# A two-block transformer kernel: row sums from the residual's addition, squared deviations from ScalarE

## What is computed

```python
def rmsnorm(x, w):
    xf = x.astype(jnp.float32)
    y = xf * lax.rsqrt(jnp.mean(xf * xf, axis=-1, keepdims=True) + EPS)
    return (y * w.astype(jnp.float32)).astype(x.dtype)

def _layer_norm(x, g, b):
    xf = x.astype(jnp.float32)
    mu = jnp.mean(xf, -1, keepdims=True)
    xc = xf - mu
    var = jnp.mean(xc * xc, -1, keepdims=True)
    y = xc * lax.rsqrt(var + NORM_EPS) * g.astype(jnp.float32) + b.astype(jnp.float32)
    return y.astype(x.dtype)

    for l in range(DEPTH_2):
        x = _layer_norm(alpha * x + 0.5 * _swiglu(x, ffn_w_gu[l, 0], ffn_w_down[l, 0]), ln_g[l, 0], ln_b[l, 0])
        ...
        x = _layer_norm(alpha * x + mix, ln_g[l, 1], ln_b[l, 1])
        x = _layer_norm(alpha * x + 0.5 * _swiglu(x, ffn_w_gu[l, 1], ffn_w_down[l, 1]), ln_g[l, 2], ln_b[l, 2])
```

## Time and profile before

| | |
|---|---|
| median of three runs | 1430.88 us |
| the profiled execution | 1435.12 us |
| its span | 1433.5 us |
| TensorE busy | 1351.0 us, 94% |
| VectorE busy | 917.1 us, 64% |
| ScalarE busy | 725.6 us, 51% |
| GpSimd busy | 93.7 us, 7% |
| mean granted clock of TensorE | 0.968 |

### The profile page before, as it was taken

The page is one execution under the profiler, slowest core; times in us unless marked ns, Lnnn a source line. Parts: engine busy times, 40 slices in busy tenths (PEclk is TensorE's granted clock), DMA queues, the critical chain, the costliest instruction groups (busy, mean ns, idle before and its releaser), DMA issues.

```text
span 1433.5 us, 20478 instructions
## 1 busy us (share of the span) xinstructions
PE 1351.0 (94%) x8221; PEld 1193.1 (83%) x8222; DVE 917.1 (64%) x1342; ACT 725.6 (51%) x1142; POOL 93.7 (7%) x137
## 2 busy tenths in 40 slices
PE   6888899998899999999899999999999999899997
PEld 6777888886788888888888888888888888888886
DVE  4787776777656658555666567656667464666556
ACT  5566455554455553564354554555553653354452
POOL 1233000000000000510000000000001400000000
PEclk9997999999999999998999999999999997999999
DMA  7333476665575664432476665666654332375661
GB/s 231 94 113 103 123 214 208 206 185 172 152 219 177 183 188 113 142 118 63 120 235 182 198 204 151 181 203 202 182 162 128 97 118 64 113 235 177 197 200 44
DMA packets 301191, 229.17 MB, mean 160 GB/s; under 512 B 13083, under 2 KB 283818, under 8 KB 301098
## 3 DMA queue, kind: packets, MB, share of 16 engines
q1 hardware_dynamic: 301082, 227.88, 52.8%
q10 hardware_dynamic: 16, 0.00, 0.0%
HBM read 226.80 MB, written 1.05 MB: 159 GB/s over the span
## 4 chain that ended last, share of the span: by engine, by line
PE 70%; DVE 15%; ACT 9%; DMA 3%; issue 2%; POOL 1%; SPq 0%; DVEq 0%; ACTq 0%
PE bank L849 20%; PE bank L783 11%; PE bank L852 10%; PE bank L784 10%; PE bank L785 10%; DVE lo_gu L1665 5%; ACT hi_gu L1316 4%; PE bank L1221 3%; DMA st_dn<-in_ffn_w_down 2%; PE bank L1190 2%; DVE lo_dn L1670 2%; PE bank L1201 1%; DVE conv L1830 1%; DVE stats L1692 1%; DVE n L1715 1%
## 5 line engine op out<-in xcount | busy, mean ns | idle before, releaser
L849 PE MATMUL bank<-xT,hi_gu 128*128 128x512 f32 x1616 | 404.8, 393 | 4.9 <-DVE lo_gu L1665 4.3
L1665 DVE TENSOR_TENSOR lo_gu<-st_gu,hi_gu 128x2048 fp32r<-128x2048 f32 (+2 forms) x146 | 323.4, 2218 | 111.9 <-ACT hi_gu L1316 111.8
L849 PEld LDWEIGHTS bank<-xT,hi_gu 128*128 128x128 f32 x1616 | 297.0, 189 | 64.4 <-DVE lo_gu L1665 6.4
L1316 ACT ACTIVATE hi_gu<-st_gu 128x2048 fp32r<-128x2048 f32 (+3 forms) x147 | 270.2, 1843 | 0.5 <-DMA st_gu<-in_ffn_w_gu 0.3
L852 PEld LDWEIGHTS bank<-xT,lo_gu 128*128 128x128 f32 x1616 | 220.8, 191 | 15.9
L852 PE MATMUL bank<-xT,lo_gu 128*128 128x256 f32 x1616 | 225.5, 282 | 0.0
L783 PE MATMUL bank<-hi_dn,actTh 128*128 128x512 f32 x436 | 172.4, 395 | 9.2 <-DVE actTl L1842 4.7
L784 PE MATMUL bank<-lo_dn,actTh 128*128 128x512 f32 x436 | 170.8, 392 | 0.0
L785 PE MATMUL bank<-hi_dn,actTl 128*128 128x512 f32 x436 | 169.7, 389 | 0.0
L1833 DVE TENSOR_TENSOR act<-act,bank 128x256 f32<-128x256 f32 x101 | 42.6, 421 | 174.2 <-ACT act L1413 174.2
L1323 ACT ACTIVATE hi_dn<-st_dn 128x1024 fp32r<-128x1024 f32 x109 | 114.6, 1056 | 67.9 <-DMA st_dn<-in_ffn_w_down 67.9
(11 more groups left out here) (270 smaller groups left out, 1823.7 us busy)
## 6 DMA issues: line engine op xcount, KB each, us to landing
st_gu<-in_ffn_w_gu SPq DMA_DIRECT2D x176, 512.0 KB, 5.2
st_dn<-in_ffn_w_down SPq DMA_DIRECT2D x109, 512.0 KB, 6.6
st_gu<-in_w_in SPq DMA_DIRECT2D x23, 1024.0 KB, 5.4
st_gu<-in_w_out SPq DMA_DIRECT2D x12, 1024.0 KB, 5.1
st_gu<-in_ffn_w_gate SPq DMA_DIRECT2D x21, 512.0 KB, 4.2
st_gu<-in_ffn_w_val SPq DMA_DIRECT2D x21, 512.0 KB, 5.5
st_gu<-in_w_in SPq DMA_DIRECT2D x10, 512.0 KB, 4.1
gb<-in_ln_g SPq DMA_DIRECT2D x6, 512.0 KB, 7.3
```

What stands on the lines that cost most here:

```text
L849: pe.matmul(b[:, :], hv[:, w, k, :], xT[:, k, :, :].rearrange("p a b -> p (a b)"), start=k == 0, stop=k == KD - 1, skip_group_check=True)
L1316: i = act.activation(high, staged, ACT.Copy)
L1665: i = dve.tensor_tensor(low, staged, high.bitcast(F32), ALU.subtract)
```

## The change

The statistics of norms 1 to 8 are computed in another way:

- `add` also writes the row sum of its half (`accum_out=row_sum`).
- A new step `centre` waits for the second half's sum and, in a layer norm, makes minus_mean of both.
- `bn_stats` and `bn_aggr` fall away for these norms. A new function `deviation` on ScalarE squares both halves of x, with minus_mean as the bias in a layer norm, and accumulates the squares over the row (`square_sum`). The squared elements go to act32 and nonlin, which nothing reads in that stretch.
- ms is one small operation on the two sums of squares. It now stands in `normalize`, behind n. The division by 1024 is the scale of ScalarE's root.
- In `norm` both additions of the second block now stand ahead of the first block's xT (before: one). In `norm_behind_out` the second block's first addition stands ahead of the first block's xT (norms 4 and 7; before: behind both weight chunks).

No activation table load is added: ScalarE's program has 32 in both kernels. GpSimd's and SP's programs are unchanged.

```diff
+            def deviation(i, m):
+                for h in range(2):
+                    act.wait_ge(x_added.sem, x_added[i, m, h])
+                    junk, xs = (act32, nonlin)[h][:, :, :].rearrange("p a b -> p (a b)"), x[:, m, h * HALF:(h + 1) * HALF]
+                    if NORMS[i][2]:
+                        act.wait_ge(mean_done.sem, mean_done[i, m])
+                        p = act.activation(junk, xs, ACT.Square, bias=minus_mean[:, m:m + 1], accum_out=square_sum[:, m, h:h + 1])
+                    else:
+                        p = act.activation(junk, xs, ACT.Square, accum_out=square_sum[:, m, h:h + 1])
+                p.then_inc(squares_summed.sem, squares_summed.one((i, m)))
+                act.wait_ge(var_done.sem, var_done[i, m])
+                act.activation(sd[:, m:m + 1], ms[:, m:m + 1], ACT.Sqrt, scale=1.0 / D).then_inc(dev_done.sem, dev_done.one((i, m)))
...
             def norm_behind_out(i, f):
-                act.wait_ge(var_done.sem, var_done[i, 0])
-                act.activation(sd[:, 0:1], ms[:, 0:1], ACT.Sqrt).then_inc(dev_done.sem, dev_done.one((i, 0)))
+                deviation(i, 0)
                 for j in range(2):
                     weights_high(CHUNK_NO["ffn", f, j])
                 turned_high(i, 0)
-                act.wait_ge(var_done.sem, var_done[i, 1])
-                act.activation(sd[:, 1:2], ms[:, 1:2], ACT.Sqrt).then_inc(dev_done.sem, dev_done.one((i, 1)))
+                deviation(i, 1)
                 turned_high(i, 1)
...
             def add(i, m, h):
-                dve.scalar_tensor_tensor(out=xs, in0=xs, scalar=NORMS[i][0], in1=bank[2 * m + h][:, :], op0=ALU.mult, op1=ALU.add).then_inc(
-                    x_added.sem, x_added.one((i, m, h)))
+                dve.scalar_tensor_tensor(out=xs, in0=xs, scalar=NORMS[i][0], in1=bank[2 * m + h][:, :], op0=ALU.mult, op1=ALU.add,
+                                         accum_out=row_sum[:, m, h:h + 1]).then_inc(x_added.sem, x_added.one((i, m, h)))
+            def centre(i, m):
+                dve.wait_ge(x_added.sem, x_added[i, m, 1])
+                if NORMS[i][2]:
+                    dve.tensor_scalar(minus_mean[:, m:m + 1], row_sum[:, m, 0:1], row_sum[:, m, 1:2], -1.0 / D, ALU.add, ALU.mult).then_inc(
+                        mean_done.sem, mean_done.one((i, m)))
...
             def variance(i, m):
-                own()
-                dve.bn_aggr(mv[:, m, :], stats[:, m, :, :].rearrange("p a b -> p (a b)")).then_inc(own_v.sem, own_v.one())
-                own()
-                if NORMS[i][2]:
-                    k = dve.tensor_scalar(ms[:, one], mv[:, m, 1:2], NORMS[i][1], None, ALU.add)
...
+                    dve.wait_ge(squares_summed.sem, squares_summed[i, m])
+                    k = dve.tensor_scalar(ms[:, one], square_sum[:, m, 0:1], square_sum[:, m, 1:2], NORMS[i][1] * D, ALU.add, ALU.add)
...
             def normalize(i, m):
                 if centred:
+                    dve.wait_ge(mean_done.sem, mean_done[i, m])
                     for h, hs in halves:
-                        dve.scalar_tensor_tensor(out=n[:, m, hs], in0=x[:, m, hs], scalar=mv[:, m, 0:1], in1=gb[:, 0, hs],
-                                                 op0=ALU.subtract, op1=ALU.mult).then_inc(own_v.sem, own_v.one())
+                        dve.scalar_tensor_tensor(out=n[:, m, hs], in0=x[:, m, hs], scalar=minus_mean[:, m:m + 1], in1=gb[:, 0, hs],
+                                                 op0=ALU.add, op1=ALU.mult).then_inc(own_v.sem, own_v.one())
+                variance(i, m)
                 dve.wait_ge(dev_done.sem, dev_done[i, m])
...
             def norm(i):
+                for m in range(M):
+                    for h in range(2):
+                        add(i, m, h)
+                    centre(i, m)
+                    if m == 1 and i != LAST:
+                        turned_low(i, 0)
+                    normalize(i, m)
+                if i != LAST:
+                    turned_low(i, 1)
+
+            def norm_behind_out(i, f):
                 for h in range(2):
                     add(i, 0, h)
...
+                centre(i, 0)
                 normalize(i, 0)
                 weights_low(CHUNK_NO["ffn", f, 0])
+                add(i, 1, 0)
                 if f:
                     turned_low(i, 0)
                     weights_low(CHUNK_NO["ffn", f, 1])
-                for h in range(2):
-                    add(i, 1, h)
-                    statistics(i, 1, h)
-                variance(i, 1)
+                add(i, 1, 1)
+                centre(i, 1)
                 normalize(i, 1)
```

29 lines of the change are left out of this document (8 added, 21 removed).

## The result

| | before | changed |
|---|---|---|
| median of 20 executions each, on one chip | 1434.05 us | 1421.01 us |
| lowest and highest | 1421.86, 1440.82 | 1412.90, 1426.30 |
| the profiled execution | 1435.12 us | 1412.90 us |
| its span | 1433.5 us | 1411.4 us |
| its mean granted clock | 0.968 | 0.983 |

The changed kernel is faster by 0.8%: ratio 0.9918, interval 0.9896 to 0.9941. The forecast was 1429.1 us and a range that ended at 1424. So it was wrong, and what it lacked is a gain.

What follows compares the result with a forecast made beforehand. TensorE, busy 94% of the span, was taken as the bound, so relief counts only where it waits. Norm terms 1.0 + 2 x 0.4 + 2 x 0.5 - 0.3 + 0.1 - 0.85 = 1.75 us took 1430.88 to 1429.1 us; range 1424 to 1438.

Steps and rivals of the forecast that it cites:

- Read of the accumulator: VectorE, behind each addition that also writes its row sum: 0.08 us more, bounds 0 and 0.24.
- Norm 8: Kernel's end, a bare VectorE chain: scaling after 3.86 us in place of 4.35; gain 0.5 per block, 1.0 in all.
- Norm 5: First block's xT starts 0.26 us later, behind scalings, both additions and minus_mean; loss 0.3 us.
- Norm 1: Second block's squares queue on ScalarE behind copies of the first block's transposes; scaling at 170.25, not 169.41; loss 0.85 us.
- Norms 3 and 6: Second block, set by ScalarE's hi_out and squares: scaling starts at 555.87 in place of 556.24; gain 0.4 us each.
- Norms 4 and 7: First product 0.8 us late, taken out of the 1.97 us wait; second block's scaling earlier; gain 0.5 us each.
- Norm 2: Uncentred: ms 0.8 us earlier, the second addition costs that again; xT at 361.15, not 361.25; gain 0.1 us.
- Sum: All eight norms' gains and losses added: 1.75 us gained, from 25 us of VectorE work removed.
- case A: The main case: work moved off an engine waited for only in places; 1426 to 1436 us, chance 76%.
- Rival B: VectorE's accumulating addition is slow, 0.68 us more each: 13.4 us lost, 1442.5 us; chance 8%.
- rival C: Shorter waits in norms 3, 4, 6 and 7 spare TensorE's half-speed clock windows: some 8 us gained, 1421 us; chance 10%.

Runs made afterwards that it cites:

- e2: The changed kernel, unchanged, run again for a second trace; ratio 0.9902 to the kernel before.
- e16: The kernel before, unchanged, run again for its spread and one more trace; ratio 1.0009.
- e1: The kernel before, unchanged, run again for a second trace; ratio 1.0005.
- e5: The kernel before with five more matmuls in the middle of FFN 1, which move everything behind them in time; ratio 0.9991.
- e14: The kernel before with two matmuls of zeros filling TensorE's wait ahead of the transposes of the mixers' later units; ratio 0.9979.
- e13: The changed kernel with two unread bn_stats behind ms in the second block of norms 3, 4, 6 and 7; ratio 0.999 to the kernel before.
- e11: The changed kernel with two unread bn_stats ahead of ms in the second block of norms 3, 4, 6 and 7; ratio 0.9901 to the kernel before.
- e10: The changed kernel, unchanged, run once more; ratio 0.9917 to the kernel before.
- e7: The kernel before with matmuls of zeros, four to eight at a place, where TensorE waits in norms 2 to 7; ratio 0.9922.

## Why the prediction was wrong

- **Read of the accumulator, 0.08 per addition**: mis-sized. Between two additions it costs 0.01 to 0.02; but an addition behind a scaling starts 0.22 later than before. minus_mean took 0.21, not 0.15.
- **Norm 8, 1.0**: too large, 10.02 - 9.32 = 0.70. **Norm 5, -0.3**: TensorE's waits add up to 3.18 where they were 2.99, so -0.2.
- **Norm 1, -0.85**: 2.55 - 3.52 = -0.97. The forecast's own terms give 168.35 + 1.30 + 0.69 = 170.34, not 170.25, and so -0.93.
- For the others I take the time from the norm's first addition to TensorE's first product with the second block, in traces that have no half speed between the two. **Norms 3 and 6, 0.4 each**: norm 3 took 558.11 - 544.75 = 13.36 us and takes 559.24 - 546.38 = 12.86; 0.5 each, about right. **Norms 4 and 7, 0.5 each**: norm 4 took 705.36 - 684.70 = 20.66 and takes 703.31 - 683.09 = 20.22 in e2; 0.44, right. xT was late as forecast (1.93), and the transposes' wait came down to 0.67, forecast 0.7. **Norm 2, 0.1**: 370.01 - 355.48 = 14.53 became 371.66 - 357.36 = 14.30; 0.23.
- **Sum, 1.75**: 0.70 - 0.97 - 0.2 + 2 x 0.5 + 2 x 0.44 + 0.23 = 1.64 us. So the direct working, case A, was right to 0.1 us in sum; that it is so close is partly luck, as its terms miss by up to 0.3 us and cancel. The means of full length (-0.8 and -0.3, each with an error of 1) are too coarse to confirm more than that it is small. Rival B is out: an addition takes 0.68 us, as before.
- **The step that failed** is the weighing of rival C: "the total idle time per norm hardly changes", and "the two rows show that the same waits fall either way". The first looked at the total per norm, which fell by 0.3 (norms 3 and 6) and 0.4 us (4 and 7), and not at how it is split: the last wait was halved, or brought down to a third. The second took two windows of one execution for the rule. Norm 3 lost nothing there, but 3.4 us in e16. At norm 6, every trace with a last wait of 1.75 us or more has a window: six of six (given, e1, e5, e14, e16 and e13), five in forms of the kernel before and one in the changed kernel with its wait put back. With 1.35 or less, or filled, none of eleven has one. That holds for norm 6: at norm 3 the same six traces have waits of 1.77 to 1.85 us and only e16 has a window, so a long wait isn't enough by itself. The total of the waits seems not to be what counts: e11, one trace, has 1.46 + 1.26 = 2.72, as much as the 0.87 + 1.84 = 2.71 of before, and no window. C's mechanism was right and its price (8 us) came near what the norms gave. Its chance of 10% was too low. What the runs showed in place of the unchanged clock is 12.9 and 12.7 us less lost (e2, e10), beside which the 1.64 us of direct gain hardly count.
- **What no rival held** is the mixers' ends, 15 us in the profiled execution. I had looked at the clock beside the norms alone, though the page shows them. Its part 2, the granted clock in 40 slices of the kernel before, has an 8 at 645 to 681 us and a 7 at 1183 to 1219:

```profile
PEclk9997999999999999998999999999999997999999
```

A third of the loss is there. With them in view C would have been worth 8 to 23 us, and the range would have reached 1429 - 23 = 1406.

The Trainium skill (TensorE: Matmul & The Clock Gate, section Why this matters for your kernels) speaks of gaps between bursts of matmuls as what lets the clock fall. The runs here agree: filling the waits (e7) took 14.7 us of loss away, and making them longer again (e13) brought 8 back.

**Still open**: why the falls at the mixers' ends are common before and rare after, and with them a large part of the gain (15.4 of the 22 us between the two profiled executions). Filling the waits there takes them away (e14), but filling the norms alone does too, in e7's trace and by the loss of its 8 executions. So what happens at the norms, or when, seems to have its say 90 us later. How is not shown. The moved kernel e5 doesn't settle it: 3 of its 12 executions lost more than 40 us, and 4 of the 25 of the kernel before on that chip. Nor was it tried which of the six norms counts for that, or why norm 3 is mostly spared.
